# Recurrence: three units of the gate projection ahead of the first tile, the others three places up, weights split one chunk ahead

## The reference, cut to what matters

```python
proj = h @ w_in
q, k, v, zf, zi, zq, zg, za, zh = jnp.split(proj, cuts, axis=-1)
...
f = lb + (1.0 - lb) * jax.nn.sigmoid(zf)
log_f, kh = jnp.log(f), 1.0 - f
def step(S, inp):                       # a chunk of the sequence
    b = jnp.cumsum(lfc, axis=1)
    o_inter = jnp.einsum('bthk,bhkv->bthv', qc * jnp.exp(b), S)
    ...                                 # scores within the chunk, masked, times v
    S_new = jnp.exp(bC)[..., None] * S + jnp.einsum('bshk,bshv->bhkv', kd, vc)
o_h = rms_norm(o_h, hg_norm_g) * jax.nn.silu(zg)
merged = jax.nn.sigmoid(za) * (att @ w_att_branch) + jax.nn.sigmoid(zh) * (o_h @ w_hg_branch)
```

## Time and profile before

| | us |
|---|---|
| median of 3 runs | 4749.6 |
| lowest and highest | 4746.81, 4753.24 |
| the profiled execution | 4748.39 |
| its span, first to last instruction | 4746.7 |
| recurrence in it, first DMA issue to last | 837.35 to 1191.58 |

### The profile page before, as it was taken

The page is one execution under the profiler, slowest core; times in us unless marked ns, Lnnn a source line. Parts: engine busy times, 40 slices in busy tenths (PEclk is TensorE's granted clock), DMA queues, the critical chain, the costliest instruction groups (busy, mean ns, idle before and its releaser), DMA issues.

```text
span 4746.7 us, 66778 instructions
## 1 busy us (share of the span) xinstructions
PE 4405.9 (93%) x26658; PEld 2287.3 (48%) x26658; DVE 2357.4 (50%) x4402; ACT 1148.7 (24%) x1671; POOL 1017.0 (21%) x542
## 2 busy tenths in 40 slices
PE   4999687799587989999999999999999999999998
PEld 3675342466235435555555544444444444444443
DVE  4232112676454038999999535555555333233235
ACT  4233110343342023343344310101101111111112
POOL 0000000331010000000000046556556323223222
PEclk8999798898898989999999999999999999999999
DMA  5232535321642148899877687676677344444443
GB/s 182 88 110 74 156 96 192 126 89 49 208 148 90 48 116 226 262 265 294 255 206 221 198 174 152 144 147 145 145 147 152 87 102 96 91 99 100 91 93 102
DMA packets 1028830, 684.61 MB, mean 144 GB/s; under 512 B 847010, under 2 KB 926970, under 8 KB 1020347
## 3 DMA queue, kind: packets, MB, share of 16 engines
q1 hardware_dynamic: 1019092, 596.09, 49.5%
q10 hardware_dynamic: 4896, 71.31, 3.6%
q0 software_dynamic: 4592, 13.64, 0.8%
HBM read 438.53 MB, written 205.97 MB: 136 GB/s over the span
## 4 chain that ended last, share of the span: by engine, by line
PE 61%; DVE 2%; DMA 1%; SPq 0%; issue 0%; ACT 0%; POOL 0%; DVEq 0%; ACTq 0%; POOLq 0%
PE ex_psy L2727 30%; PE ex_psa L2687 29%; PE rt_psg L2710 1%; PE rt_psg L2711 1%; DMA ex_u<-in_peer_u_dram 1%; SPq L2206 0%; DVE rt_hotg L2476 0%; DVE ex_acc L2634 0%; DVE rt_hote L2472 0%; DVE ex_ulo L2447 0%; DVE ex_acc L2613 0%; DVE rt_same L2546 0%; DVE rt_same L2538 0%; DVE rt_same L2544 0%; DVE ex_acc L2603 0%
## 5 line engine op out<-in xcount | busy, mean ns | idle before, releaser
L2727 PE MATMUL ex_psy<-ex_vhi,ex_wboth 128*128 128x512 f16 x4352 | 1323.1, 379 | 9.9 <-issue 8.7
L2687 PE MATMUL ex_psa<-h_hi,ex_uth 128*128 128x512 f16 (+1 forms) x3072 | 878.8, 317 | 22.4 <-DMA ex_utl<-ex_ulo 21.0
L2687 PE MATMUL ex_psa<-h_lo,ex_uth 128*128 128x512 f16 (+1 forms) x3072 | 880.3, 317 | 0.0
L2299 POOL TENSOR_SCALAR ex_v<-ex_v 128x1024 f32<-128x1024 f32 x128 | 408.5, 3191 | 2197.8 <-DMA ex_v<-in_peer_v_dram 2197.8
L2727 PE MATMUL ex_psy<-ex_vlo,ex_wboth 128*128 128x512 f16 x2304 | 874.2, 379 | 0.0
L2687 PE MATMUL ex_psa<-h_hi,ex_utl 128*128 128x512 f16 (+1 forms) x3072 | 866.7, 317 | 0.0
L2727 PEld LDWEIGHTS ex_psy<-ex_vhi,ex_wboth 128*128 128x128 f16 x4352 | 426.2, 98 | 520.9 <-issue 11.8
L2596 DVE TENSOR_TENSOR ex_acc<-ex_acc,ex_psy 128x512 f32<-128x512 f32 x540 | 364.5, 684 | 481.2 <-PE ex_psy L2727 480.6
L2331 ACT ACTIVATE ex_wa<-ex_psa 128x512 f32<-128x512 f32 (+1 forms) x384 | 178.7, 472 | 1069.4 <-PE ex_psa L2687 973.7
L2687 PEld LDWEIGHTS ex_psa<-h_hi,ex_uth 128*128 128x128 f16 x3072 | 292.4, 98 | 263.7 <-DMA ex_utl<-ex_ulo 21.5
L2585 DVE SCALAR_TENSOR_TENSOR ex_wa<-ex_wa,ex_gate 128x1088 f32<-128x1088 f32 x128 | 193.5, 1512 | 442.1 <-ACT ex_wa L2331 426.7
(11 more groups left out here) (359 smaller groups left out, 5632.2 us busy)
## 6 DMA issues: line engine op xcount, KB each, us to landing
gate_all<-rt_stage ACTq DMA_DIRECT2D x34, 2048.0 KB, 8.1
ex_gate<-gate_all SPq DMA_DIRECT2D x128, 544.0 KB
ex_u<-in_peer_u_dram SPq DMA_DIRECT2D x128, 512.0 KB, 4.8
ex_v<-in_peer_v_dram SPq DMA_DIRECT2D x128, 512.0 KB, 7.9
act_all<-ex_wa SPq DMA_DIRECT2D x80, 544.0 KB, 3.5
ex_wa<-act_all SPq DMA_DIRECT2D x80, 544.0 KB, 3.8
ad_w<-in_ada_w_dram SPq DMA_DIRECT2D x8, 2048.0 KB, 10.1
pa_w<-in_w_in_dram SPq DMA_DIRECT2D x10, 1024.0 KB, 7.7
```

The lines of the kernel that those rows point to most:

```text
L2299: nc.gpsimd.tensor_scalar(v[s][:, :], v[s][:, :], SPLIT, None, ALU.mult).then_inc(v_sc, 1)
L2687: mm = nc.tensor.matmul(ps_a[:, at:at + e - a], x[s][:, k, :], h[:, k, a:e], start=(k == 0 and j == 0), stop=(k == KD - 1 and j == 2))
L2727: mm = nc.tensor.matmul(ps_y[n % YB][:, :], w, v_[:, a * 512:(a + 1) * 512], start=(j == 0), stop=(j == len(mms) - 1))
```

## The change

The tensors, banks and instructions stay the same, and so does their number. What moves:

- TensorE runs units 0, 1 and 2 of chunk 0 ahead of tile 0. The slots of tile n then hold units 3 and 4 of chunk n and 0, 1 and 2 of chunk n + 1 (`unit_at`). In tile 7 only slots 0 and 1 are left. A unit 1 that falls into a slot cut in two is done whole at the slot's first piece, so it stands behind step 1.
- ScalarE rounds chunk 0 ahead of the logarithm of tile 0 and chunk 1 behind it, and empties units 0 and 1 before tile 0. Tile n rounds chunk n + 2.
- VectorE forms the remainder of chunk 0 between the two inversions of tile 0, and that of chunk 1 behind the corrected logarithm. Tile n forms that of chunk n + 2.
- SyncE loads chunks 2 and 3 in tile 0, and chunk n + 3 in tile n.

```diff
--- before.py
+++ after.py
@@ -1249,7 +1249,9 @@
     fi_in, tmp_done = [pr.sem(f"hg_fi{s}") for s in range(2)], pr.sem("hg_tmp")
     w_in, z_stored = ([pr.sem(f"hg_{n}{s}") for s in range(2)] for n in ("win", "zstored"))
     w_hi_done, w_lo_done, filled, emptied = (pr.sem(f"hg_{n}") for n in ("whi", "wlo", "filled", "emptied"))
-    ZC, UNITS = 2 * P, 5
+    ZC, UNITS, AHEAD_UNITS = 2 * P, 5, 3
+    ALL_UNITS = PT * UNITS
+    unit_at = lambda n, slot: n * UNITS + AHEAD_UNITS + slot
     with ExitStack() as cx:
         sb = lambda name, shape: cx.enter_context(nc.sbuf_tensor(f"hg_{name}", shape, F32))
         ps = lambda name, shape: cx.enter_context(nc.psum_tensor(f"hg_{name}", shape, F32))
@@ -1307,9 +1309,10 @@
             def tile(n, s, rows, ch, kind):
                 if n:
                     store_gates(n - 1, 1 - s)
-                if n + 2 < PT:
-                    sp.wait_ge(w_lo_done, n + 1)
-                    load_weights(n + 2, s)
+                for c in (2, 3) if n == 0 else (n + 3,):
+                    if c < PT:
+                        sp.wait_ge(w_lo_done, c - 1)
+                        load_weights(c, c % 2)
                 if n + 2 <= PT:
                     sp.wait_ge(squared, n + 1)
                     load(n + 2, s, P if n + 2 < PT else NS)
@@ -1359,7 +1362,10 @@
                     act.wait_ge(filled, (c - 1) * UNITS)
                 nc.scalar.activation(w_hi[c % 2][:, :, :], w[c % 2][:, :, :], ACT.Copy, scale=SPLIT).then_inc(w_hi_done, 1)
 
-            def empty(c, u):
+            def empty(q):
+                if q >= ALL_UNITS:
+                    return
+                c, u = divmod(q, UNITS)
                 act.wait_ge(filled, c * UNITS + u + 1)
                 if u == 0 and c >= 2:
                     act.wait_ge(z_stored[c % 2], c // 2 * 32)
@@ -1381,18 +1387,17 @@
                 after = NS if n == PT - 1 else P
                 if kind == "p":
                     exponentials(n + 1, 1 - s, after)
-                if n:
-                    empty(n - 1, 4)
+                empty(unit_at(n, -1))
                 act.wait_ge(k_tr, n + 1)
                 nc.scalar.copy(kt[:, :, r], ps_cn[:, :].rearrange("p (h t) -> p h t", h=HH)[:, :, r]).then_inc(k_t, 1)
                 if kind == "p":
-                    empty(n, 0)
+                    empty(unit_at(n, 0))
                     logs(n + 1, after)
-                    empty(n, 1)
-                    if n + 1 < PT:
-                        high(n + 1)
-                    empty(n, 2)
-                    empty(n, 3)
+                    empty(unit_at(n, 1))
+                    if n + 2 < PT:
+                        high(n + 2)
+                    empty(unit_at(n, 2))
+                    empty(unit_at(n, 3))
                 act.wait_ge(inter, n * 4 + nch + 2)
                 act.wait_ge(sg_done, n + 1)
                 nc.scalar.activation(osq[:, :, r], ps_o[:, :, r], ACT.Square).then_inc(squared, 1)
@@ -1403,8 +1408,11 @@
 
             act.sem_inc(emptied, 2)
             exponentials(0, 0, P)
+            high(0)
             logs(0, P)
-            high(0)
+            high(1)
+            empty(0)
+            empty(1)
             tiles(tile, 0)
 
         @block.gpsimd
@@ -1506,8 +1514,8 @@
                     dve.wait_ge(s_done, q + 1)
                 if kind == "p":
                     invert_gate(n + 1, 1 - s, after)
-                if n + 1 < PT:
-                    low(n + 1)
+                if n + 2 < PT:
+                    low(n + 2)
                 dve.wait_ge(msum, n + 1)
                 nc.vector.tensor_scalar(x_t(r), ps_cn[:, :].rearrange("p (h t) -> p h t", h=HH)[:, :, r],
                                         1.0 / HK, EPS, ALU.mult, ALU.add).then_inc(ms, 1)
@@ -1531,17 +1539,23 @@
             dve.sem_inc(inter, 2)
             dve.sem_inc(o_free, 1)
             invert_forget(0, P)
+            low(0)
             invert_gate(0, 0, P)
             correct_log(0, P)
-            low(0)
+            low(1)
             tiles(tile, 0)
 
         @block.tensor
         def _(pe):
-            def fill(c, u, ks):
-                if c >= PT:
+            def fill(q, ks):
+                if q >= ALL_UNITS:
                     return
-                q, bank = c * UNITS + u, ps_z[(c * UNITS + u) % 2]
+                c, u = divmod(q, UNITS)
+                bank = ps_z[q % 2]
+                if u == 1:
+                    if ks[0]:
+                        return
+                    ks = range(0, KD)
                 if ks[0] == 0:
                     pe.wait_ge(w_lo_done, c + 1)
                     pe.wait_ge(emptied, q + 1)
@@ -1562,7 +1576,7 @@
                 for h in range(HH):
                     nc.tensor.matmul(ps_ct[:, h, 0:rows + nch], lf[r, h * HK:(h + 1) * HK], tri, start=True, stop=True)
                 nc.tensor.matmul(ps_cn[r, :], tri[:, r], lf[r, :], start=True, stop=True).then_inc(sums, 1)
-                fill(n, 0, range(0, KD))
+                fill(unit_at(n, 0), range(0, KD))
                 pe.wait_ge(k_done, n + 1)
                 for h in range(HH):
                     mm = nc.tensor.transpose(ps_cn[:, h * P:h * P + rows], kh[s][r, h * HK:(h + 1) * HK],
@@ -1584,14 +1598,14 @@
 
                 for c in range(2):
                     increments(c)
-                fill(n, 1, range(0, KD))
+                fill(unit_at(n, 1), range(0, KD))
                 pe.wait_ge(k_t, n + 1)
                 pe.wait_ge(q_done, n + 1)
                 for h in range(HH):
                     mm = nc.tensor.matmul(ps_ct[r, h // 2, h % 2 * P:h % 2 * P + rows], kt[:, h, r], qg[s][:, h, r],
                                           start=True, stop=True)
                 mm.then_inc(a_done, 1)
-                fill(n, 2, range(0, 4))
+                fill(unit_at(n, 2), range(0, 4))
                 pe.wait_ge(am_done, n + 1)
 
                 for h in range(HH):
@@ -1608,12 +1622,14 @@
                         pe.wait_ge(tmp_done, n * 4 + c + 1)
                         increments(c + 2)
                     if c < 3:
-                        fill(n, (2, 3, 3)[c], range(4, 8) if c != 1 else range(0, 4))
+                        fill(unit_at(n, (2, 3, 3)[c]), range(4, 8) if c != 1 else range(0, 4))
                 pe.wait_ge(squared, n + 1)
                 nc.tensor.matmul(ps_cn[:, :].rearrange("p (h t) -> p h t", h=HH)[:, :, r], pr.c("ones"), osq[:, :, r],
                                  start=True, stop=True).then_inc(msum, 1)
-                fill(n, 4, range(0, KD))
-
+                fill(unit_at(n, 4), range(0, KD))
+
+            for q in range(AHEAD_UNITS):
+                fill(q, range(0, KD))
             tiles(tile, 0)
 
 
```

## The result

| us | before | after |
|---|---|---|
| median | 4750.98 (20 runs) | 4761.81 (20 runs) |
| lowest and highest | 4743.21, 4757.16 | 4756.78, 4769.72 |
| the profiled execution | 4748.39 | 4758.06 |
| its span | 4746.7 | 4756.4 |

The ratio is 1.0023, with a 95% interval of 1.0017 to 1.0029: slower by 0.23%, 10.8 us between the medians. The prediction said 4754.8, 5.2 us above before, with a range up to 4761 and 0.12 for slower by over 0.2%. It was wrong: the median lies 0.8 us above the range, and about 6 of the 10.8 us are missing from its sum.

The account below looks back on a forecast made before the run. It took the eight prompt tiles to be bound by TensorE, the sample tile by VectorE and TensorE in turn. Start 5.2, tiles 0 and tail 0 gave 5.2 us slower: median 4754.8 us, range 4746 to 4761.

Parts of the forecast that it names:

- its sum: Whole recurrence: start, tiles 0 to 6 and tail add as 5.2 + 0 + 0 = 5.2 us slower.
- The start: Ahead of tile 0: three units overrun TensorE's wait, tile 0 begins 7.0 us later, 1.8 us come back, net 5.2.
- the bound: Start of the recurrence: the latest landing of chunk 0's weight load, by 850.9.
- The 1.75 us of slow time in the sum: Ahead of tile 0: units 0 to 2 take 11.8 + 1.75 = 13.5 us.
- The work of a tile is the same 35.36 us ... Cost: 0: Tiles 0 to 6: reordered units make VectorE's state work 3.77 us later, but TensorE has 1.0 us of slack; cost 0.
- The rival that priced this place: Tiles 0 to 5: VectorE, slowed beside GpSimd's multiply, becomes the bound; 11.2 us slower at 1 us each; chance 0.13.
- a fall in tile 7: Tile 7: TensorE's clock falls near 18.6 us into the tile, 3.3 us after the dense work ends.
- The tail: Tile 7 and sample tile: keys 1.2 us earlier, then some 1.2 us lost to slow clock; net 0, bounds -2.9 and +3.0.

Follow-up runs that it names:

- the three kernels of the table: The changed kernel with the small unit in slot 1, or half or an eighth of slot 4's unit behind step 2: 4754.41, 4754.90, 4754.30 us.

## Why the prediction was wrong

**The start was right.** The load was there before the bound: chunk 0's rounding waited 1.35 us for it and began at 846.48, 10.8 us behind the stage's first DMA issue (bound 13.6). The remainder began as VectorE's inversion ended. The first unit began as the remainder ended, 16.7 us behind that issue (predicted 17.0). The multiply of GpSimd took 3.08 us beside the remainder, as predicted, and its delay hid behind the units:

```profile
846.48 1.91 ACT L1363 ACTIVATE hg_whi<-hg_w 128x2048 f16<-128x2048 f32 x1 [1.35 <-DMA hg_w<-in_w_in_dram]
...
850.11 2.23 DVE L1480 SCALAR_TENSOR_TENSOR hg_wlo<-hg_w,hg_whi 128x2048 f16<-128x2048 f32 x1
...
850.37 3.08 POOL L1437 TENSOR_TENSOR hg_f<-hg_f,hg_oml 128x512 f32<-128x512 f32 x1 [2.52 <-DVE hg_f L1466]
...
852.39 0.61 PE L1567 MATMUL hg_ps_z<-h_hi,hg_whi 128*128 128x512 f16 x1 [24.26 <-DVE hg_wlo L1480]
```

Tile 0 came 6.8 us later (predicted 7.0), and its sums at full clock gave the 1.8 us back. The 1.8 us are those of the earlier trace rows, where the first gate matmul begins 3.57 us behind the sums in tile 0 and 1.76 in tile 7. The 1.75 us of slow time in the sum were an estimate from the same 3.57 us: no run of the kernel before shows gate units ahead of tile 0. In the changed kernel the windows put the clock at 0.50 from the first unit's start, 852.4, to about 855.9, and units 0 to 2 took 13.5 us (852.39 to 865.90), 1.7 more than their 11.8 inside a tile.

**The step that failed** is "The work of a tile is the same 35.36 us ... Cost: 0". The work was the same; its speed was not. The term is 8.8 us in five tiles, in place of 0. The step asked only whether VectorE would be late for TensorE, and there it was right: the mean square came 32.3 us into the tile (predicted 32.4), the keys 4.96 into tile 1, behind an unstretched tile (906.30 after 901.34; predicted 5.3), and TensorE waited for neither. The rival that priced this place at 1.05 us more for the product beside the multiply didn't come: the logarithm's correction, behind the mean square, took 1.04 us inside a tile and not 1.74. That is 0.35 more than its 0.69. VectorE in the tile that begins at 1011.06:

```profile
1043.35 0.68 DVE L1520 TENSOR_SCALAR hg_kt<-hg_ps_cn 128x512 f32<-128x512 f32 x1
1044.07 1.04 DVE L1475 SCALAR_TENSOR_TENSOR hg_lf<-hg_x,hg_lf 128x512 f32<-128x512 f32 x1
```

Nobody was late, and the tiles were still 1.7 us longer. The section on the change gives TensorE's order in tile 7 alone; that of a tile in the middle would have shown step 2 and step 3 side by side there too. The prediction priced a fall in tile 7, "after a microsecond in which TensorE was busy for 0.83" and behind the last dense work, and it did not ask the same question of the seven tiles in which a wide half unit had left the place behind step 2.

**The tail was right in kind.** The clock fell in tile 7 at about 1142.7, 20.3 us into the tile (predicted 18.6). TensorE's last wait ahead of it, 0.78 us, ended at 1138.53; from there to the fall it was busy. A product with the state then took 1.8 us and an increment 1.97, near the 1.87 and 2.07 of the sample tile:

```profile
1140.44 1.15 PE L1596 MATMUL hg_ps_u<-hg_fi,hg_kh 32*128 32x128 f32 x8
1141.52 1.08 PE L1617 MATMUL hg_ps_o<-hg_qg,hg_sp 128*128 128x32 f32 x8
1142.53 1.97 PE L1596 MATMUL hg_ps_u<-hg_fi,hg_kh 32*128 32x128 f32 x8
1144.43 3.62 PE L1617 MATMUL hg_ps_o<-hg_qg,hg_sp 128*128 128x32 f32 x16
1148.74 2.07 PE L1627 MATMUL hg_ps_cn<-hg_osq,const 128*128 128x512 f32 x2 [0.69 <-ACT hg_osq L1403]
```

The keys came 2.0 us earlier (predicted 1.2), and the low clock at the start of the sample tile cost 0.7 (predicted 1.2): -1.3 for a predicted 0.

**The range** ended at 4761, with a stall of one us a tile in six tiles behind VectorE. That rival's 11.2 us lie near the measured 10.8, by luck: the stall didn't come, and the cause is another. The three kernels with wide work behind step 2 or the small unit back in slot 1 lie at 4754.3 to 4754.9, and their recurrences are 4.8 to 5.0 us longer than before, against 5.2 in the sum. So the forecast fits the kernel as it was imagined. In the tile shown, the one that begins at 1011.06, the only idle time of TensorE near the fall is 0.69 us, and before has the same 0.69 without a fall; so that gap alone does not decide.

## What to carry over

When a change reorders work on an engine that is hardly ever idle, look at what each stretch between two dense pieces now holds, not only at who waits for whom: here 7.7 us without a wide gate matmul cost 1.7 us in each of five tiles, with no wait but the 0.69 us that was there before. Look at the order of a tile in the middle of the loop, since that is paid in each. Work put into a wait at the start cost what it overhung (6.8 and 16.8 us for three and five units). One unit fitted and still cost 1.7 us, because forming its weights delayed the logarithm. Such work came back at the end only as far as it stood ahead of the chain that ends there: tile 7 gave 0.8 to 0.9 us back with both of its wide units ahead of the scores (the three kernels of the table), and 5.0 us with the second of them behind the scores.

## What the runs showed of the hardware

- The clock fell in five tiles of seven with the same instructions in each (0.95 over the tile, against 1.00 in the other two), and in five of eight with the units only exchanged. Why in those tiles and not in the others stays open.
- 0.65 us of wide matmuls between steps 2 and 3 prevented the fall in tiles 0 to 6, behind a half unit and the small unit (35.4 us a tile, against 37.1). One such piece behind each of steps 0 to 2, without these, did not prevent it in tile 7 of three kernels.
- In the sample tile 0.65 us a step did not raise a low clock in 20 us, and two such pieces in a row did in each of the kernels that had them at a low clock, the first time only for 3.4 us.
- Busy was no sign of a full clock. Small float32 matmuls that the profile calls busy without a break ran at clock 0.50 for 24.5 us on end, in the sample tile before. One of the seven windows of 3.5 us from 1157.0 on:

```profile
1164.00:1167.50 3.50, 3.50 (x16) 3.25 (x16) 2.07 (x3) 0.00 (x0) 0.00 (x0) 0.50 0.00 0
```
